# Fourteen of a block 1 layer's eighteen modulation units moved from the head slots to the norm and convolution mean slots, two a slot

## The chip, the cores and the metric

One Trainium2 (trn2) chip, of which the kernel uses 1 core. The metric is the device time of one execution in microseconds (us), lower is better. It is given as the median of several executions of one built kernel.

## What is computed

Two transformer-like blocks run one after the other on a sequence of 256 tokens of width 1024, in float32, each with two layers (`DEPTH = 2`). Cut to what matters here:

```python
def first_block(x, ...):
    for l in range(DEPTH):
        h = _rmsnorm(x, g_mix[l])
        proj = h @ w_in[l]                       # gates 4096, conv 512, three attentions 2560 columns
        y_a = _conformer_conv(a_in, ...)         # depthwise conv of 31 taps, layernorm, silu
        y_b = _neighbourhood_attn(norm(bq), norm(bk), bv, na_rpb[l])
        y_c = _dilated_attn(rope(norm(cq)), rope(norm(ck)), cv)
        y_d = _window_gqa_sink(rope(norm(dq)), rope(norm(dk)), dv, swa_sink[l])
        branch = einsum('bsnc,ncd->bsnd', stack(y_a, y_b, y_c, y_d), w_branch[l])
        gates = sigmoid(gate_pre + gate_b[l])
        x = x + sum(gates * branch, axis=2) @ w_out[l]
        x = x + _conv_ffn(_rmsnorm(x, g_ffn[l]), ...)
    return x

def second_block(x, c, ctx, c_ctx, w_mod, b_mod, ...):
    for l in range(DEPTH):
        m_x = silu(c) @ w_mod[l] + b_mod[l]      # modulation: 1024 x 9216, needs c alone
        m_c = silu(c_ctx) @ w_mod[l] + b_mod[l]
        ...                                      # FFN, MLA attention, FFN, all scaled by m_x, m_c
```

The modulation of block 2 depends on none of block 1's results, so it can be computed anywhere before block 2 needs it.

## The kernel before, in words

**Products.** A float32 weight tile of 1 MB (`raw`, a ring of `RAW = 4` slots) is loaded by SyncE's queue (L713), rounded by ScalarE into `whi` (helper `copy`, L1193, in `round_next`), and what the rounding left is taken by VectorE into `wlo` (L1542, in `rest_next`). TensorE then makes three products for every pair of 128-row tiles (L859 to L861 in `unit`). A *unit* of the phase `gates` is 48 such products of 256 columns into two PSUM banks `acc`. ScalarE takes the two results out with a tanh (L1374).

**Modulation.** `w_mod` is cut into 36 *modulation units* a layer, each 1 MB. A modulation unit skips the rounding: `mod_unit` (L946) multiplies `cond` by the raw tile, 8 small products into a bank; `mod_rows` (ScalarE, `copy`) copies the row to `mod_row`; `mod_turn` (TensorE, L955) turns it into columns in the same bank; `mod_out` (VectorE, L1661) adds the bias. A bank and a half of `mod_row` are used again two units later, so `mod_unit` waits for the `mod_out` of two units before. Half of layer 0's 36 units (of block 2's layer 0) are computed in block 1's layer 0, half in its layer 1; the other 36 lie in block 2's attention and are not touched.

**The slots.** Block 1's attention part is written out by hand as a list of slots (`slots_block1`), and every engine walks the same list. They are: six `prep` slots (prep 0 to prep 5), each the norm of two tiles of q or k, with rope from prep 2 on; a `mean` slot and a `var` slot for the layernorm behind the convolution; and fourteen `head` slots (head 0 to head 13), each with the scores of one head, the softmax of the one before and the value product of the one before that. Sixteen `gates` units are spread over them: prep 0, 2, 4 and mean have gates 0 to 3, heads 0 to 11 have gates 4 to 15. Within a slot each engine keeps its own written order:

- TensorE: in `prep` the sum of squares (L830), the gates unit, the rope product (L1042). In `head` the scores (L906), the turn (L955) and product (L946) of a modulation unit, the gates unit, in every second slot a further turn and product, then `weigh` (`op`, L926) and `turn_probs` (`ptp`, L915).
- ScalarE: in `prep` the squares (L1233), the root (`take_root`, L1245), the rounding of the next weights, the two tanh. In `head` the rounding, `exps` (L1286), `mod_rows`, the two tanh, the copies of `ptp` and `op`. Sqrt, tanh and exp need table loads (ACT_TABLE_LOAD) between them, exp and tanh together none.
- VectorE: in `prep` the reciprocal of the root (L1570), the scaling (L1587), `wlo`, the rope (L1771 to L1774). In `head` `peaks` (L1607 to L1618), `normalise` (L1636, L1640), `wlo`, `mod_out`, `br_lo` (L1653).

**Order of the loads.** `mod_order` puts each modulation tile into the stream of loads behind a gates tile; the ring of four slots is filled strictly in that order, and a slot is free when the tile four places before has been used.

**Eighteen units over the heads.** `mods_block1(l, k)` gives head k one unit, and heads 2, 4, 6 and 8 (`MOD_TWICE`) two. Their banks are `stat` and `rotp`, which no norm or rope needs during the heads.

```python
MOD_TWICE = (2, 4, 6, 8)
def mod_bank(u):
    return (stat, rotp)[u % 2]
```

## Time and profile before

| | |
|---|---|
| Median of 3 runs | 3140.37 us (3120.49 to 3142.45) |
| The profiled execution's own time | 3125.25 us |
| Its span, first to last instruction | 3123.5 us |
| TensorE busy | 2860.1 us (92%) |
| VectorE, ScalarE, GpSimdE busy | 1546.2, 1102.8, 70.6 us |
| Mean granted TensorE clock | 0.936 of full speed |

The profile is of one execution. The span leaves 1.75 us of the execution's time outside it. Times in rows of the trace count from the span's start. Block 1's layer 0 has its slots from about 99 to 287 us, layer 1 from about 641 to 828 us. A matmul's busy time is modelled and overlaps that of the next, so the distance between the starts of two rows is what a step costs.

### The profile page before, as it was taken

To read this page: it belongs to the slowest core of one execution; us is meant where nothing else is said; L and a number is where in the kernel's file an instruction comes from. 1 tells how busy PE (TensorE), PEld (TensorE's weight loads), DVE (VectorE), ACT (ScalarE), POOL (GpSimd) and SP (SyncE) were. 2 spreads that over 40 slices of the span, in tenths; PEclk is the share of its full clock that TensorE was granted. 3 is DMA by queue.
4 is the path that set the end of the run, shared out by engine and by line. 5 is a ranking of instruction groups with operands and counts; after the bars stand their busy time and mean duration, and the time that the engine had idled before them with its cause. 6 is when DMAs were issued, how large, how long until landed. Compare 5 with 4: busy or idle time off the path is not lost.

```text
span 3123.5 us, 41599 instructions
## 1 busy us (share of the span) xinstructions
PE 2860.1 (92%) x16697; PEld 2360.6 (76%) x16697; DVE 1546.2 (50%) x2230; ACT 1102.8 (35%) x1527; POOL 70.6 (2%) x97
## 2 busy tenths in 40 slices
PE   6899799889889989999799998999979999799897
PEld 6677799867779968888574565888858888656897
DVE  5755676775568553333433235333353333543655
ACT  4543464455346442121333223222132121433433
POOL 3000100100100000000000000000000000000000
PEclk9899899999989989999898698999989999789999
DMA  7376365627546532433234432242322423334563
GB/s 199 108 227 219 108 182 153 193 95 249 197 136 183 153 97 80 114 86 94 69 80 138 137 119 67 70 113 82 101 68 74 122 82 100 92 112 132 139 191 92
DMA packets 613569, 394.44 MB, mean 126 GB/s; under 512 B 47691, under 2 KB 609543, under 8 KB 613157
## 3 DMA queue, kind: packets, MB, share of 16 engines
q1 hardware_dynamic: 609424, 383.03, 41.6%
q0 software_dynamic: 2960, 7.75, 1.0%
q8 instruction: 112, 1.84, 0.3%
q10 hardware_dynamic: 1029, 1.47, 0.1%
q14 instruction: 44, 0.36, 0.0%
HBM read 391.16 MB, written 1.05 MB: 126 GB/s over the span
## 4 chain that ended last, share of the span: by engine, by line
PE 84%; DVE 10%; ACT 3%; issue 1%; DVEq 1%; DMA 0%; ACTq 0%; POOL 0%
PE acc L859 12%; PE acc L860 11%; PE acc L861 11%; PE scores L859 6%; PE scores L860 6%; PE scores L861 6%; PE scores L906 3%; PE acc L877 3%; PE acc L878 3%; PE acc L879 3%; PE scores L877 3%; PE scores L878 3%; PE scores L879 3%; PE op L926 2%; DVE rstd L1570 2%; DVE wlo L1542 2%
## 5 line engine op out<-in xcount | busy, mean ns | idle before, releaser
L1193 ACT ACTIVATE whi<-raw 128x2048 fp32r<-128x2048 f32 (+2 forms) x326 | 565.8, 1736 | 895.2 <-PE acc L861 287.3
L859 PE MATMUL acc<-h_hi,whi 128*128 128x256 f32 (+1 forms) x2372 | 801.5, 338 | 84.8 <-DVE h_lo L1581 48.3
L1542 DVE TENSOR_TENSOR wlo<-raw,whi 128x2048 fp32r<-128x2048 f32 (+2 forms) x325 | 674.6, 2076 | 214.5 <-ACT whi L1193 213.9
L860 PE MATMUL acc<-h_lo,whi 128*128 128x256 f32 (+1 forms) x2372 | 778.6, 328 | 0.0
L861 PE MATMUL acc<-h_hi,wlo 128*128 128x256 f32 (+1 forms) x2372 | 777.6, 328 | 0.0
L859 PEld LDWEIGHTS acc<-h_hi,whi 128*128 128x128 f32 x2372 | 462.9, 195 | 173.4 <-issue 78.4
L860 PEld LDWEIGHTS acc<-h_lo,whi 128*128 128x128 f32 x2372 | 465.9, 196 | 37.1 <-issue 2.5
L861 PEld LDWEIGHTS acc<-h_hi,wlo 128*128 128x128 f32 x2372 | 464.8, 196 | 37.4
L859 PE MATMUL scores<-h_hi,whi 128*128 128x256 f32 (+1 forms) x992 | 334.7, 337 | 0.0
L860 PE MATMUL scores<-h_lo,whi 128*128 128x256 f32 (+1 forms) x992 | 334.0, 337 | 0.0
L861 PE MATMUL scores<-h_hi,wlo 128*128 128x256 f32 (+1 forms) x992 | 333.7, 336 | 0.0
L859 PEld LDWEIGHTS scores<-h_hi,whi 128*128 128x128 f32 x992 | 186.6, 188 | 22.3 <-issue 0.2
L861 PEld LDWEIGHTS scores<-h_hi,wlo 128*128 128x128 f32 x992 | 186.8, 188 | 21.6
L860 PEld LDWEIGHTS scores<-h_lo,whi 128*128 128x128 f32 x992 | 186.7, 188 | 21.6
L877 PE MATMUL acc<-a_hi,whi 128*128 128x256 f32 (+1 forms) x528 | 181.2, 343 | 8.1 <-DVE wlo L1542 8.1
L878 PE MATMUL acc<-a_lo,whi 128*128 128x256 f32 (+1 forms) x528 | 180.4, 342 | 0.0
L879 PE MATMUL acc<-a_hi,wlo 128*128 128x256 f32 (+1 forms) x528 | 180.3, 341 | 0.0
L877 PE MATMUL scores<-a_hi,whi 128*128 128x256 f32 (+1 forms) x528 | 179.2, 339 | 0.0
L879 PE MATMUL scores<-a_hi,wlo 128*128 128x256 f32 (+1 forms) x528 | 178.8, 339 | 0.0
L878 PE MATMUL scores<-a_lo,whi 128*128 128x256 f32 (+1 forms) x528 | 178.8, 339 | 0.0
L1871 DVE TENSOR_TENSOR a_hi<-sg,acc 128x512 f32 (+3 forms) x48 | 29.9, 622 | 262.4 <-PE acc L861 262.4
L1871 DVE TENSOR_TENSOR a_hi<-sg,scores 128x512 f32 (+3 forms) x40 | 24.9, 622 | 221.8 <-PE scores L861 221.8
(274 smaller groups left out, 3305.3 us busy)
## 6 DMA issues: line engine op xcount, KB each, us to landing
raw<-in_ffn_w_in_dram SPq DMA_DIRECT2D x176, 512.0 KB, 5.0
raw<-in_w_mod_dram SPq DMA_DIRECT2D x72, 1024.0 KB, 5.1
raw<-in_w_in_dram SPq DMA_DIRECT2D x62, 1024.0 KB, 5.3
raw<-in_w_up_dram SPq DMA_DIRECT2D x88, 512.0 KB, 4.9
raw<-in_ffn_w_out_dram SPq DMA_DIRECT2D x64, 704.0 KB, 4.6
raw<-in_w_down_dram SPq DMA_DIRECT2D x32, 704.0 KB, 4.7
raw<-in_w_out_dram SPq DMA_DIRECT2D x16, 1024.0 KB, 5.3
raw<-in_w_branch_dram SPq DMA_DIRECT2D x8, 1024.0 KB, 6.4
```

Of the source, the lines that this page charges most:

```text
L859: pe.matmul(bank, wh, hi[:, c0 + k, 0:width], start=(k == 0), stop=False)
L860: pe.matmul(bank, wh, lo[:, c0 + k, 0:width], start=False, stop=False)
L861: ins = pe.matmul(bank, wl, hi[:, c0 + k, 0:width], start=False, stop=(k == ph.shape[0] - 1))
L877: pe.matmul(bank, wh, hi[:, c0 + k, 0:width], start=(k == 0), stop=False)
L878: pe.matmul(bank, wh, lo[:, c0 + k, 0:width], start=False, stop=False)
L879: ins = pe.matmul(bank, wl, hi[:, c0 + k, 0:width], start=False, stop=(k == FH - 1))
L906: ins = pe.matmul(bank[:, t * w:(t + 1) * w], q_, k_, start=(e == 0), stop=(e == len(terms) - 1))
L926: ins = pe.matmul(op_[job["rows"], 0:w], v, job["prt"][:, b % 2, kt * w:(kt + 1) * w], start=(kt == 0), stop=(kt == nk - 1))
L1193: return act.activation(out_, in_, ACT.Copy, **kw)
L1542: dve.tensor_tensor(wlo[:, s % 2, 0:el], raw[:, slot, 0:el], f32(whi[:, s % 2, 0:el]), ALU.subtract).then_inc(s_lo, 1)
L1570: dve.reciprocal(rstd[:, 0:w_], root[:, 0:w_]).then_inc(s_rstd, 1)
L1871: dve.tensor_tensor(hi, sg2[:, b, 0:T], bank_of(ph, j, 1, 4)[:, 0:T], ALU.mult).then_inc(s_accfree, 1)
```

## The change

Of a layer's eighteen modulation units, fourteen are now issued in the slots prep 0 to prep 5 and mean, two in each, and four in heads 1, 3, 5 and 7. In the prep and mean slots the units come at the end of the slot on TensorE; their copies, turns and outputs stand in the *next* slot (the list `late`). In the heads too, a unit is now issued at the end of its slot, and its copy, turn and output come in the next slot. Units in prep and mean slots use the banks `scores0` and `scores1`, which no attention uses there; the scores of head 0 now wait for their last output. The tiles stand earlier in the stream of loads.

Cut to its core (`...` marks what is left out):

```diff
-MOD_TWICE = (2, 4, 6, 8)
+MOD_HEADS = (1, 3, 5, 7)
...
+        rounded = 0
+        for (kind, k, gate), units in zip(slots_block1(), mods_block1(l)):
+            rounded = rounded if gate is None else gate + 1
+            behind = (f"1.{l}.gates", rounded) if rounded < 16 else (f"1.{l}.branch", 0)
+            given.setdefault(behind, []).extend((0, e) for e in units)
+            u += len(units)
...
+def mods_block1(l):
+    out_, u = [], l * MOD_HALF
+    for kind, k, gate in slots_block1():
+        units = 2 if kind in ("prep", "mean") else 1 if kind == "head" and k in MOD_HEADS else 0
+        out_.append(list(range(u, u + units)))
+        u += units
+    return out_
...
         def mod_bank(u):
+            if u < MOD_UNITS and u % MOD_HALF < MOD_HALF - len(MOD_HEADS):
+                return sp_[u % 2]
             return (stat, rotp)[u % 2]
...  TensorE
+                late = []
+                for (kind, k, gate), here in zip(slots1, mods_block1(l)):
...
-                            pe.wait_ge(s_rpbm, 4 * (l + 1))
+                            pe.wait_ge(s_modout, n("mod"))
                             scores(0, jobs[0])
...
-                    if kind == "head":
-                        mine = mods_block1(l, k)
-                        if k == 0:
-                            pe.wait_ge(s_cond, 2)
-                            pe.wait_ge(s_root, n("norm"))
-                        else:
-                            mod_turn()
-                        mod_unit(0, mine[0])
+                    for u in late:
+                        mod_turn()
                     if gate is not None:
                         unit(nm + "gates", gate, None, h1_hi, h1_lo, SEQ, plain(256))
-                    if kind == "head":
-                        for u in mine[1:]:
-                            mod_turn()
-                            mod_unit(0, u)
...
                     if kind == "head":
                         attend(jobs, k)
...
+                    for u in here:
+                        mod_unit(0, u)
+                    late = here
...  ScalarE
                         squares(norm_heads(l, k))
+                    if kind == "var":
+                        squares(norm_conv(l), [(s_conv, 2 * l + 2)])
+                    if kind != "head":
+                        for u in late:
+                            mod_rows()
+                    if kind == "prep":
                         take_root(norm_heads(l, k))
...
                     if kind == "head":
-                        mod_rows()
+                        for u in late:
+                            mod_rows()
+                    late = here
...  VectorE
                     if gate is not None:
                         rest_next(nm + "gates", gate, None)
-                    if kind == "head" and k >= 1:
+                    for u in late:
                         mod_out()
+                    late = here
```

TensorE, block 1's layer 0, from the sum of squares of prep 1 on. Before, where only the gates unit of prep 2 (its 48 products on `acc1` and `acc0` are left out here) stands between the sums of squares and the rope product:

```order
L830 MATMUL stat<-sq,shared 128x512 [waits s_root,s_sq] x2
...
L1042 MATMUL rotp<-qk,t1 128x512 [waits s_plain]
L830 MATMUL stat<-sq,shared 128x512 [waits s_root,s_sq]
L1042 MATMUL rotp<-qk,t1 128x512 [waits s_roped,s_plain]
L830 MATMUL stat<-sq,shared 128x512 [waits s_root,s_sq]
```

Now, the same place up to the sum of squares of prep 2 (its two turns and its gates unit follow):

```order
L836 MATMUL stat<-sq,shared 128x512 [waits s_root,s_sq]
L961 MATMUL scores0<-shared,mod_row 128x2 [waits s_modrow]
L961 MATMUL scores0<-shared,mod_row 128x2
L961 MATMUL scores1<-shared,mod_row 128x2 [waits s_modrow]
L961 MATMUL scores1<-shared,mod_row 128x2
L952 MATMUL scores0<-raw,cond 32x256 [waits s_modout,s_raw2]
L952 MATMUL scores0<-raw,cond 32x256 x7
L952 MATMUL scores1<-raw,cond 32x256 [waits s_modout,s_raw3]
L952 MATMUL scores1<-raw,cond 32x256 x7
L836 MATMUL stat<-sq,shared 128x512 [waits s_root,s_sq]
```

The sum of squares of prep 2 stood right behind that of prep 1; now it stands behind two modulation products that wait for VectorE (`s_modout`).

ScalarE, the same layer, from the squares of prep 1 to the root of prep 2. Before:

```order
L1233 ACTIVATE sq<-qk 128x512 [waits s_sum]
L1245 ACT_TABLE_LOAD [waits s_rstd]
L1245 ACTIVATE root<-stat,eps 128x512 [waits s_sum]
L1233 ACTIVATE sq<-qk 128x512 [waits s_sum]
L1245 ACTIVATE root<-stat,eps 128x512 [waits s_rstd,s_sum]
```

Now:

```order
L1237 ACTIVATE sq<-qk 128x512 [waits s_sum]
L1197 ACTIVATE mod_row<-scores0 128x256 [waits s_modmm]
L1197 ACTIVATE mod_row<-scores1 128x256 [waits s_modmm]
L1249 ACT_TABLE_LOAD [waits s_rstd]
L1249 ACTIVATE root<-stat,eps 128x512 [waits s_sum]
L1237 ACTIVATE sq<-qk 128x512 [waits s_sum]
L1197 ACTIVATE mod_row<-scores0 128x256 [waits s_modt,s_modmm]
L1197 ACTIVATE mod_row<-scores1 128x256 [waits s_modt,s_modmm]
L1249 ACTIVATE root<-stat,eps 128x512 [waits s_rstd,s_sum]
```

Each root now stands behind two copies that wait for the modulation products (`s_modmm`), and in prep 1 the table load stands behind them too.

TensorE in the heads, from the end of head 1 to the first product of the gates unit of head 2 (`ptp` of head 0, then the scores of head 3). Before:

```order
L915 MATMUL ptp<-shared,pr1 128x128 [waits s_turned,s_prob]
L915 MATMUL ptp<-shared,pr1 128x128 x3
L906 MATMUL scores1<-qk 128x256 [waits s_exp]
L906 MATMUL scores1<-qk 128x256
L955 MATMUL rotp<-shared,mod_row 128x2 [waits s_modrow]
L955 MATMUL rotp<-shared,mod_row 128x2
L946 MATMUL stat<-raw,cond 32x256 [waits s_modout,s_raw0]
L946 MATMUL stat<-raw,cond 32x256 x7
```

Now:

```order
L921 MATMUL ptp<-shared,pr1 128x128 [waits s_turned,s_prob]
L921 MATMUL ptp<-shared,pr1 128x128 x3
L952 MATMUL stat<-raw,cond 32x256 [waits s_modout,s_raw3]
L952 MATMUL stat<-raw,cond 32x256 x7
L912 MATMUL scores1<-qk 128x256 [waits s_exp]
L912 MATMUL scores1<-qk 128x256
L961 MATMUL stat<-shared,mod_row 128x2 [waits s_modrow]
L961 MATMUL stat<-shared,mod_row 128x2
```

Before, the turn belonged to the unit multiplied ahead of head 1's gates unit; now it belongs to the one multiplied just ahead of the scores, with only the scores between product and turn.

## Rows read from the trace of the kernel before

**Rows 1.** The page: the span, and the chain that ended last by engine.

```profile
span 3123.5 us, 41599 instructions
...
PE 84%; DVE 10%; ACT 3%; issue 1%; DVEq 1%; DMA 0%; ACTq 0%; POOL 0%
```

**Rows 2.** Windows: layer 0's preps, heads; layer 1's; 11 us of loads. The first line names the columns.

```profile
core 0: us, PE busy (x) PEld busy (x) DVE busy (x) ACT busy (x) POOL busy (x), PEclk, DMA share, GB/s
98.80:156.60 57.80, 44.27 (x249) 33.94 (x247) 42.39 (x35) 31.62 (x38) 0.00 (x0) 0.85 0.22 74
156.60:287.30 130.70, 127.71 (x1060) 103.72 (x1057) 67.33 (x141) 64.52 (x126) 0.00 (x0) 0.99 0.72 234
641.00:697.20 56.20, 41.25 (x247) 31.96 (x245) 41.73 (x33) 29.63 (x35) 0.00 (x0) 0.91 0.23 75
697.20:828.30 131.10, 127.67 (x1061) 104.02 (x1057) 67.37 (x141) 64.52 (x126) 0.00 (x0) 0.99 0.72 231
...
711.00:722.00 11.00, 11.00 (x101) 9.74 (x102) 5.20 (x9) 5.59 (x11) 0.00 (x0) 1.00 0.89 282
```

**Rows 3.** ScalarE's timeline, preps 0 and 1: start us, us, what, [idle before, releaser].

```profile
107.03 0.47 ACT L1374 ACTIVATE gates<-acc,par 128x256 f32<-128x256 f32 x1 [1.41 <-PE acc L861]
107.40 0.62 ACT L1233 ACTIVATE sq<-qk 128x512 f32<-128x512 f32 x1
108.03 1.28 ACT L1245 ACT_TABLE_LOAD   x1
109.33 0.69 ACT L1245 ACTIVATE root<-stat,eps 128x512 f32<-128x512 f32 x1
```

**Rows 4.** Timeline of VectorE: reciprocal and scaling of prep 1, `wlo`; then prep 5.

```profile
110.11 3.35 DVE L1570 RECIPROCAL rstd<-root 128x512 f32<-128x512 f32 x1 [1.59 <-ACT root L1245]
113.56 0.75 DVE L1587 SCALAR_TENSOR_TENSOR qk<-qk,par,rstd 128x512 f32<-128x512 f32 x1
...
118.52 2.29 DVE L1542 TENSOR_TENSOR wlo<-raw,whi 128x2048 fp32r<-128x2048 f32 x1
...
140.17 1.75 DVE L1570 RECIPROCAL rstd<-root 128x256 f32<-128x256 f32 x1
```

**Rows 5.** Timeline of TensorE in preps 2 to 4: rope product and sum of squares.

```profile
118.83 1.02 PE L1042 MATMUL rotp<-qk,t 128*128 128x512 f32 x2
...
127.11 2.08 PE L1042 MATMUL rotp<-qk,t 128*128 128x512 f32 x2 [5.92 <-DVE qk L1587]
128.98 1.92 PE L830 MATMUL stat<-sq,shared 128*128 128x512 f32 x2
```

**Rows 6.** Timeline of TensorE from head 4's end into head 5, and that unit's end.

```profile
205.45 1.08 PE L926 MATMUL op<-prt,v 128*64 128x256 f32 x4
206.46 0.66 PE L915 MATMUL ptp<-shared,pr 128*128 128x128 f32 x4
207.05 1.13 PE L906 MATMUL scores<-qk 64*128 64x256 f32 x4
208.34 0.61 PE L955 MATMUL stat<-shared,mod_row 128*128 128x2 f32 x4 [0.16 <-ACT mod_row L1193]
208.87 1.07 PE L946 MATMUL rotp<-raw,cond 128*32 128x256 f32 x16
209.87 0.39 PE L859 MATMUL acc<-h_hi,whi 128*128 128x256 f32 x1
...
215.76 1.08 PE L926 MATMUL op<-prt,v 128*64 128x256 f32 x4
```

**Rows 7.** Timeline of ScalarE in head 5.

```profile
210.35 0.91 ACT L1286 ACTIVATE pr<-sm,npeak 128x256 f32<-128x256 f32 x2 [0.27 <-DVE npeak L1618]
211.17 0.36 ACT L1193 ACTIVATE mod_row<-rotp 128x256 f32<-128x256 f32 x1
```

**Rows 8.** The page's DMA issues: the modulation tiles, us from issue to landing.

```profile
raw<-in_w_mod_dram SPq DMA_DIRECT2D x72, 1024.0 KB, 5.1
```

**Rows 9.** Timeline of TensorE in layer 1's head 9: product, gates unit, `op`.

```profile
792.44 1.07 PE L946 MATMUL rotp<-raw,cond 128*32 128x256 f32 x16 [1.03 <-DMA raw<-in_w_mod_dram]
...
800.84 1.08 PE L926 MATMUL op<-prt,v 128*64 128x256 f32 x4
```

More of the change, by code:

```diff
@@ L237, in mod_order @@
     for l in range(DEPTH):
-        for kind, k, gate in slots_block1():
-            if kind == "head":
-                behind = (f"1.{l}.gates", gate + 1) if gate is not None and gate < 15 else (f"1.{l}.branch", 0)
-                units = mods_block1(l, k)
-                given.setdefault(behind, []).extend((0, e) for e in units)
-                u += len(units)
+        rounded = 0
[4 more added lines that the diff above has]
+            u += len(units)
     assert u == MOD_UNITS
@@ L252, in mods_block2 @@
     return range(MOD_AHEAD) if l == 0 else range(MOD_AHEAD, MOD_UNITS)
-def mods_block1(l, k):
-    first = l * MOD_HALF + k + sum(1 for e in MOD_TWICE if e < k)
-    return list(range(first, first + (2 if k in MOD_TWICE else 1)))
+def mods_block1(l):
[5 more added lines that the diff above has]
+    return out_
 def slots_block1():
@@ L1045, in _ @@
                         attend(jobs, k)
-                mod_turn()
+                    if kind == "prep" and k == 0:
+                        pe.wait_ge(s_cond, 2)
+                        pe.wait_ge(s_rpbm, 4 * (l + 1))
+                    if kind == "head" and k == 0:
+                        pe.wait_ge(s_root, n("norm"))
+                    for u in here:
+                        mod_unit(0, u)
+                    late = here
                 n("job", 12)
@@ L1349, in _ @@
                 jobs = jobs_block1(l)
-                for kind, k, gate in slots1:
+                late = []
+                for (kind, k, gate), here in zip(slots1, mods_block1(l)):
                     if kind == "prep":
@@ L1727, in _ @@
                 jobs = jobs_block1(l)
-                for kind, k, gate in slots1:
+                late = []
+                for (kind, k, gate), here in zip(slots1, mods_block1(l)):
                     if kind == "prep":
@@ L1760, in _ @@
                         attend_rest(jobs, k)
-                        for u in mods_block1(l, k)[1:]:
-                            mod_out()
                     if kind == "prep":
@@ L1774, in _ @@
                             dve.tensor_tensor(pair, pair, rt, ALU.add).then_inc(s_roped, 1)
-                mod_out()
                 if l == DEPTH - 1:
```

5 lines of the change are left out of this document (removed).

## The prediction, written before the changed kernel had run

> **What bounds the kernel now.** I read the page first: 84% of the chain that ended last is TensorE, 10% VectorE, DMA nothing [rows 1]. So moving TensorE's work pays only where it moves into idle time of TensorE that nothing else needs. The windows by stage come next [rows 2]. They split each of block 1's layers in two. In the heads (130.70 us in layer 0, 131.10 in layer 1, from the first gates unit of head 0 to the first branch unit) TensorE is busy 127.7 us: the heads are bound by TensorE, and work taken out of them shortens them. In the prep, mean and var slots (57.80 and 56.20 us) TensorE is busy 44.27 and 41.25 us, VectorE 42.39 and 41.73: nobody is full, and the trace shows why. It is a ping-pong. ScalarE takes a root [rows 3], VectorE a reciprocal of 3.35 us and a scaling [rows 4], and TensorE sits idle for 5.92 us in front of a rope product that waits for the scaling [rows 5]. Before, this ping-pong ran partly ahead: as the order shows, a prep without a gates unit puts nothing between its own sum of squares and root and those of the next.
>
> **What the change takes out of the heads.** The number of modulation units is the same. One costs 1.00 us for the product (208.87 to 209.87) and 0.53 for the turn (208.34 to 208.87) [rows 6]. Fourteen leave: 14 x 1.53 = 21.4 us, of which about 0.4 was hidden in overlaps, so 21.0. The idle 0.9 us behind head 0's gates unit is covered (that unit starts later against the softmax than before), and a gates unit that ran at the half clock in the heads of each layer cost 1.5 us more; I count 1.3 of it as gone. Against that, in heads 12 and 13 the short chain of `op`, `ptp` and copies was partly filled by two units, and what they leave is idle, 1.1 us. Together -21.0 - 0.9 - 1.3 + 1.1 = -22.1 us a layer. At the most it is -23.6 (nothing hidden, 21.4 + 2.2); at the least, if the tail keeps all of its last two units' time (3.1 us), -20.
>
> **What it puts back into the heads.** In heads 2, 4, 6 and 8 a turn now stands right behind the scores, and its product only one place ahead of them. The turn needs the copy `mod_row`, and ScalarE makes that copy only after `exps` of this head. In head 5 of before the chain is: `op` ends about 0.07 us after `ptp` starts, so it ended at 206.53 [rows 6]; `exps` runs at 210.35, `mod_row` at 211.17 to 211.53 [rows 7]. The copy is there 5.0 to 5.2 us behind `op`. TensorE arrives at the turn after `ptp` 0.59, the product 1.00 and the scores 1.06 [rows 6], 2.6 us behind `op`. So it waits 2.6 us, four times: +10.4 us a layer. Behind the waiting turn stand the gates unit, `op` and `ptp`; their inputs are ready, so the wait is a plain loss. Before, the product lay a whole gates unit ahead of its turn, and the wait was 0.16 us [rows 6]. Bounds: 0 (if ScalarE's chain moves forward by as much) and 3.5 a time. The heads net: -22.1 + 10.4 = -11.7 us a layer.
>
> **What it does to the preps.** Each slot now closes a ring: the root stands behind the copies of the pair, these behind the pair's products, these behind the rope product and the `mod_out` of VectorE, these behind the scaling, and that behind the root. I add up from one pair's end to the next. The links, from rows:
> - Last product to next root: 1.72 us where ScalarE loads a table (copy 0.4, load 1.29, rest latency) [rows 3]; 1.1 where it does not, since TensorE's sum of squares (1.02 [rows 5]) now stands behind the pair.
> - Root to the end of scaling: 0.78 (109.33 to 110.11), 3.45 (to 113.56), 0.75: 4.98, and what follows on VectorE starts 0.08 sooner, 4.90 behind the root [rows 3, 4]. `wlo` 2.2 (2.29, less the overlap with the next) [rows 4]; a `mod_out` is some 0.15, which is small either way.
> - A pair of products 2.07, a turn 0.55, a gates unit 5.85 (209.87 to 215.76) [rows 6], a rope product 1.0 [rows 5].
>
> Layer 0, starting from the end of gates unit 0 at 106.99 (its tanh starts at 107.03 [rows 3]):
> - prep 0: two products, to 109.0.
> - prep 1: 1.72 + 4.90 + 0.2 + 2.07 = 8.9, to 117.9.
> - prep 2: here TensorE itself is the longest: sum of squares 1.05, two turns 1.1, unit 5.85, rope 0.9, pair 2.0 = 10.9, to 128.8. (VectorE needs 1.1 + 4.90 + 2.2 + 0.15 = 8.4 and is ready before the rope product ends.)
> - prep 3: 1.72 + 4.98 + 1.0 + 2.07 = 9.8, to 138.6.
> - prep 4, like prep 2: 10.9, to 149.5.
> - prep 5, 256 wide (reciprocal 1.75 [rows 4]): 1.72 + 2.9 + 0.7 + 2.07 = 7.4, to 156.9.
> - mean: mean product 1.0, turns 1.1, unit 5.85, pair 2.0 = 9.95, to 166.8.
> - var: 1.72 to the root, 4.35 through reciprocal, scaling, bias and the last `mod_out`, for which head 0's scores now wait, 1.05 for them: to 173.9.
>
> Before, head 0's gates unit began at 156.6 [rows 2]. So the preps grow by 17.3 us in layer 0. Layer 1 took some 0.8 us less than layer 0 for the same stretch and gets the same links, so +18.1: mean +17.7. Bounds: nothing of the ring lies on the path, then only the `mod_out` and copies, about +2; or each step is serial, every slot with its unit, rope, reciprocal and pair one behind the other, +30.
>
> One rule of the Trainium skill speaks on a link of this ring. The trace shows the table load at 108.03 with 1.28 us and the root at 109.33, 0.02 us behind it [rows 3], so a link costs 1.30. ScalarE: Activation LUTs, section What ACT_TABLE_LOAD costs, says that each switch also costs a drain of about 1380 ns, 2.66 us in all. By that, four links a layer (prep 1, 3, 5, var) would be 1.38 longer and the kernel 11 us slower than my sum; by the row they are not. I go by the row.
>
> **The clock.** The granted clock is 0.85 in layer 0's preps against 0.99 in the heads [rows 2], and the rows say what comes before it falls: behind 5.92 us of idle the rope product takes 2.08 instead of 1.02 and the sum of squares 1.92 instead of 1.02 [rows 5], the level of 1.2 instead of 2.4 GHz. That is 2.0 us. In my schedule TensorE has idle stretches of 4.8 us (prep 1), 4.6 (prep 3), 2.9 (prep 5) and 3.9 (var). I charge three of them with 2.0 us each, since what follows (pair, sum of squares, turns, unit) is now on the path: +6.0 a layer, bounds 0 and 11. In the heads a gates unit behind a wait of 1.03 us and a product took some 7.4 us (the product starts at 792.44, so the unit at 793.44, `op` at 800.84) [rows 9] instead of 5.89: 1.5. The four new waits of 2.6 us stand in a stretch of light work (`op`, `ptp`, product, scores, turn); I charge half of them: +3.0, bounds 0 and 6.
>
> **Loads.** The preps now take 14 modulation tiles beside their gates tiles. Walking the ring of four slots with 5.1 us from issue to landing [rows 8], each tile is there 3 us or more before its product: the closest is the second tile of prep 1, whose slot comes free with the `wlo` of gates 1 at about 108.5, so landed at 113.6, and used at 117. The heads have held 234 GB/s over 130 us and 282 over 11 us [rows 2]; 14 + 4 MB in some 75 us is 250. I charge nothing. What it costs without that cover: see the rivals.
>
> **The sum.** A layer: +17.7 (preps) - 11.7 (heads) + 6.0 + 3.0 (clock) = +15.0 us; two layers +30.0. On the profiled execution's 3125.25 that is 3155.3. This execution is 15 us below the median of 3140.37 in a spread of 22 us; I put the change on the median: 3170.4 us, +0.96%. Block 2's modulation is untouched, and the branch stage starts with the same waits.
>
> **The rivals.** A measurement of this kernel can tell about 1%, 31 us, from no change.
> - *The preps hide the pairs* (the other side). If the ring is not closed in practice because ScalarE's root of the next slot mostly waited for VectorE anyway, the preps grow by 2 us and the heads still give 11.7 less 3.0: -6.7 a layer, 3127 us. For it: 13 to 15 us of TensorE idle in each layer's preps [rows 2]. Against: they lie in front of products that wait for the scaling, and the order puts each root behind the pair of the slot before. It decides once the root of prep 2 comes within 2 us of prep 1's scaling. With the waits in the heads also missing it is -1.0% and more.
> - *The clock does not fall more often than before*: only 6.0 a layer, +12: 3152 us. For it: the pairs also fill idle time.
> - *The turns in the heads do not wait*: 10.4 + 3.0 less a layer, +3: 3144 us. Against: rows 7.
> - *The loads bound the preps*: 18 tiles one behind the other at 5.1 [rows 8] are 92 us against the 75 of my schedule, +17 a layer: 3204 us. Against: 282 GB/s with several in flight [rows 2].
> - *Every light stretch ends at the half clock*, the upper bounds of both clock terms, +8 a layer: 3186 us.
>
> Of the clock, TensorE: Matmul & The Clock Gate, section HAM oscillation, warns that idle gaps before bursts of products keep bringing back the half clock; that is this last rival's mechanism, and the trace agrees for the gap of 5.92 us.
>
> **How the numbers follow.** Chances: forecast 0.56, preps hide 0.12, clock stays 0.13, turns do not wait 0.06, loads 0.06, full clock cost 0.07. The forecast's own range is +18 to +42 us, and half of it lies above +31. Slower by over 1%: 0.29 of the forecast + 0.06 + 0.07 = 0.42. Faster by over 1%: 0.05, the far part of the first rival. The rest, 0.53, is within 1%. The range leaves out most of the first rival and the loads: 3143 to 3195.
>
> **What would show each step.** In the changed profile: the time from gates unit 0's end to head 0's gates unit (49.6 before, 67 to 73 if right); the heads from there to the first branch unit (130.7 before, 119 to 122); turns waiting for ScalarE's `mod_row` about 2.6 us, four times a layer; the root of prep 2 waiting for TensorE's sum of squares, some 8 us behind the root of prep 1; the granted clock in the preps near 0.85 still; TensorE waiting for no modulation tile. The prediction is wrong if the preps grow by less than 10 us a layer, or if the turns find their row ready.

## The result, and the profile after

The changed kernel takes 3165.21 us (median of 4 runs, 3163.92 to 3177.59); the kernel before, run beside it, 3130.43 (4 runs, 3117.01 to 3142.45). The ratio is 1.0121, with a 95% interval of 1.0063 to 1.0179: slower by about 1.2%. The forecast was 3170.4, with 3143 to 3195 as its range. A total can land in a range that wide by luck, so the terms matter more than the total, and two of them were not right. Of all executions reported here two ran in a slower state, at a mean granted clock of 0.81 (3300.64 us, one of the kernel before, and 3333.87 us, one of e8_fill_preps), and no median or ratio counts them.

The profiled execution of the changed kernel took 3165.55 us. Its page, beside [rows 1]:

```profile
span 3163.8 us, 41601 instructions
...
PE 85%; DVE 9%; ACT 3%; issue 1%; DVEq 1%; ACTq 0%; POOL 0%
```

The span is 40.3 us longer for two more instructions, and the shares of the chain have hardly moved. The page alone can't say where the time went. The windows can. I divided each layer of block 1 at the same three instructions in every trace: the end of gates unit 0, the first product of head 0's gates unit, the first product of the branch stage. Windows of the kernel before with these bounds, preps of layer 0, preps of layer 1, then everything behind layer 1's heads (the columns are those of [rows 2]; its heads are in [rows 2], as 130.70 and 131.10 us):

```profile
106.99:156.59 49.60, 36.07 (x195) 27.34 (x195) 35.50 (x29) 25.47 (x31) 0.00 (x0) 0.83 0.25 85
648.33:697.17 48.84, 33.89 (x195) 25.71 (x194) 35.59 (x29) 25.35 (x31) 0.00 (x0) 0.90 0.27 87
828.27:3123.45 2295.18, 2130.52 (x11076) 1709.34 (x11076) 1015.49 (x1419) 705.67 (x939) 16.73 (x13) 0.93 0.38 108
```

The same windows of the changed kernel: preps and heads of layer 0, preps and heads of layer 1, the rest.

```profile
106.72:180.07 73.35, 55.75 (x458) 38.71 (x458) 39.69 (x48) 33.27 (x47) 0.00 (x0) 0.83 0.81 258
180.07:311.02 130.95, 116.03 (x794) 99.49 (x793) 63.38 (x121) 57.76 (x110) 0.00 (x0) 0.91 0.39 129
669.34:743.01 73.67, 55.62 (x458) 38.82 (x458) 39.67 (x48) 33.37 (x47) 0.00 (x0) 0.84 0.80 257
743.01:874.19 131.18, 116.25 (x795) 99.72 (x793) 63.39 (x122) 57.68 (x110) 0.00 (x0) 0.91 0.39 129
874.19:3163.75 2289.56, 2117.36 (x11076) 1703.92 (x11076) 1015.12 (x1418) 705.79 (x939) 16.75 (x13) 0.93 0.38 108
```

Three things are to be read here. The preps grew by 23.8 and 24.8 us a layer. The heads, in whose windows the trace has 266 products fewer, did not shrink at all: 130.95 and 131.18 us. Their TensorE is busy 11.7 us less than before and idle for the rest, and the granted clock in them fell from 0.99 to 0.91. And the rest of the kernel, which the change doesn't touch, is 8.6 us shorter (5.6 behind layer 1's heads, 2.7 between the two layers, 0.3 before), so 48.9 us of loss in the two layers show as 40.3.

**The ring in the preps.** TensorE's waits in layer 0's preps; the fence shows every stretch of TensorE there with an idle time in front of it, and the three rows around the first:

```profile
108.51 1.13 PE L836 MATMUL stat<-sq,shared 128*128 128x512 f32 x2
109.47 0.95 PE L961 MATMUL scores<-shared,mod_row 128*128 128x2 f32 x8
115.55 3.64 PE L952 MATMUL scores<-raw,cond 128*32 128x256 f32 x32 [5.12 <-DVE mods L1671]
119.12 2.08 PE L836 MATMUL stat<-sq,shared 128*128 128x512 f32 x2
...
137.46 2.07 PE L1039 MATMUL rotp<-qk,t 128*128 128x512 f32 x2 [4.96 <-DVE qk L1597]
...
157.70 1.22 PE L1039 MATMUL rotp<-qk,t 128*128 128x256 f32 x2 [3.30 <-DVE qk L1597]
...
178.06 2.09 PE L912 MATMUL scores<-qk 64*128 64x256 f32 x8 [4.22 <-DVE mods L1671]
```

Four waits, 5.12, 4.96, 3.30 and 4.22 us: the four of the forecast's walk (4.8, 4.6, 2.9, 3.9). None waits for a tile from DMA. Behind each, the next products run at the half clock in this profile: a pair of modulation products takes 3.64 us instead of 1.93, and the sum of squares 2.08 instead of 1.13. ScalarE, beside [rows 3], shows the same ring from its side:

```profile
108.65 0.38 ACT L1197 ACTIVATE mod_row<-scores 128x256 f32<-128x256 f32 x1 [0.48 <-PE scores L952]
109.05 1.28 ACT L1249 ACT_TABLE_LOAD   x1
110.35 0.69 ACT L1249 ACTIVATE root<-stat,eps 128x512 f32<-128x512 f32 x1
...
117.54 0.38 ACT L1197 ACTIVATE mod_row<-scores 128x256 f32<-128x256 f32 x1 [5.99 <-PE scores L952]
119.25 0.38 ACT L1197 ACTIVATE mod_row<-scores 128x256 f32<-128x256 f32 x1 [1.32 <-PE scores L952]
121.23 0.69 ACT L1249 ACTIVATE root<-stat,eps 128x512 f32<-128x512 f32 x1 [1.60 <-PE stat L836]
```

ScalarE is idle for 5.99 us until the pair's first product arrives, and the next root follows the last one by 10.9 us (110.35 to 121.23). Between them VectorE's reciprocal and scaling take the same times as in [rows 4], and then come the two small outputs that free the banks:

```profile
111.13 3.35 DVE L1580 RECIPROCAL rstd<-root 128x512 f32<-128x512 f32 x1 [2.88 <-ACT root L1249]
114.58 0.75 DVE L1597 SCALAR_TENSOR_TENSOR qk<-qk,par,rstd 128x512 f32<-128x512 f32 x1
115.25 0.22 DVE L1671 TENSOR_TENSOR mods<-scores,par 128x4 f32<-128x4 f32 x2
```

So the pair starts only once these outputs are written (115.25 to 115.47), behind a reciprocal of 3.35 us that has nothing to do with them.

**The heads.** TensorE at the turn of head 2, beside [rows 6]:

```profile
195.57 1.13 PE L912 MATMUL scores<-qk 64*128 64x256 f32 x4
199.19 0.61 PE L961 MATMUL stat<-shared,mod_row 128*128 128x2 f32 x4 [2.49 <-ACT mod_row L1197]
...
200.25 0.41 PE L865 MATMUL acc<-h_hi,whi 128*128 128x256 f32 x1
...
204.81 0.28 PE L865 MATMUL acc<-h_hi,whi 128*128 128x256 f32 x1
```

TensorE waits 2.49 us for `mod_row`, whose copy stands behind `exps` on ScalarE, as in [rows 7] (the first line is one of the two exponentials of `exps`):

```profile
197.78 0.51 ACT L1290 ACTIVATE pr<-sm,npeak 128x256 f32<-128x256 f32 x1 [0.26 <-DVE npeak L1628]
198.78 0.36 ACT L1197 ACTIVATE mod_row<-stat 128x256 f32<-128x256 f32 x1
```

The four waits of layer 0 are 2.49, 2.63, 2.63 and 3.06 us, together 10.8. And the gates unit behind each pays once more: its first products come every 0.21 us, later ones every 0.12 (0.41 and 0.28 us each, as they overlap). From first gates product to `op`, the units of heads 2, 4, 6 and 8 take 7.4, 7.4, 8.4 and 8.0 us; those of the other heads 5.8 to 5.9. Head 0's unit, behind the wait of 4.22 us, starts at the half clock too and takes 7.1 to the next scores.

### The profile page after: what moved, and what is told of

Same layout as the page of the kernel before. It is cut to its first block, busy times and chain, and to the rows that moved or that the text cites. A ratio compares the mean times of both kernels' runs of the same rounds, so it can differ in the third digit from the quotient of the medians.

```text
span 3163.8 us, 41601 instructions
## 1 busy us (share of the span) xinstructions
PE 2864.0 (91%) x16697; PEld 2370.7 (75%) x16697; DVE 1547.5 (49%) x2230; ACT 1105.2 (35%) x1527; POOL 69.7 (2%) x97
## 4 chain that ended last, share of the span: by engine, by line
PE 85%; DVE 9%; ACT 3%; issue 1%; DVEq 1%; ACTq 0%; POOL 0%
PE acc L865 12%; PE acc L867 12%; PE acc L866 12%; PE scores L865 6%; PE scores L867 6%; PE scores L866 6%; PE scores L912 4%; PE acc L883 3%; PE acc L885 3%; PE acc L884 3%; PE scores L885 3%; PE scores L883 3%; PE scores L884 3%; PE op L932 3%; DVE rstd L1580 2%
## 5 line engine op out<-in xcount | busy, mean ns | idle before, releaser
L883 PE MATMUL acc<-a_hi,whi 128*128 128x256 f32 (+1 forms) x528 | 180.3, 341 | 8.0 <-DVE wlo L1552 8.0
L1880 DVE TENSOR_TENSOR a_hi<-sg,scores 128x512 f32 (+3 forms) x40 | 24.8, 621 | 220.7 <-PE scores L867 220.7
```

The costliest lines, as they stand in the source:

```text
L883: pe.matmul(bank, wh, hi[:, c0 + k, 0:width], start=(k == 0), stop=False)
L1880: dve.tensor_tensor(hi, sg2[:, b, 0:T], bank_of(ph, j, 1, 4)[:, 0:T], ALU.mult).then_inc(s_accfree, 1)
```

## The experiments

All times are medians; ratios are against the kernel before on the same chip, with 95% intervals. Kernels e1 to e4 share 32 runs of it (3125.23 us); e6, e7, e8 and the changed kernel again share 16 (3121.19); e5 stands against 7 (3115.28). Stages come from the one profiled execution of each, and without another word "the changed kernel" means its first profile.

### The heads: product and copy put back ahead of the gates unit

e1_heads_old moves the four head units back to the place they had before, within the same slots; the preps stay as changed.

```diff
  TensorE
                     for u in late:
                         mod_turn()
+                    if kind == "head":
+                        if k == 0:
+                            pe.wait_ge(s_root, n("norm"))
+                        for u in here:
+                            mod_unit(0, u)
                     if gate is not None:
                         unit(nm + "gates", ...)
...
-                    for u in here:
-                        mod_unit(0, u)
+                    if kind != "head":
+                        for u in here:
+                            mod_unit(0, u)
  ScalarE
                     if kind == "head":
-                        for u in late:
+                        for u in here:
                             mod_rows()
```

> Undoes the order in the heads alone: the four units of heads 1, 3, 5, 7 are multiplied ahead of their own slot's gates unit and copied in that slot, so that their turn comes a whole gates unit later. The preps stay as changed. Theory (the turns' waits, and the half clock behind them, eat the heads' gain): no turn waits, the gates units of heads 2, 4, 6, 8 take 5.95 us instead of 7.45 to 8.4, the heads take 112 us a layer instead of 131, and the kernel 3165 - 38 = 3127 us. Rival (the clock falls in the heads because they hold less work in all, whatever the turns do): waits gone but the units stay at 7.5 to 8.4, heads 121, 3146 us.

Measured: 3132.52 us, ratio 1.0027 (1.0002 to 1.0052). Layer 0's heads (layer 1's take 111.19):

```profile
180.10:291.77 111.67, 107.56 (x794) 91.28 (x793) 63.43 (x121) 57.68 (x110) 0.00 (x0) 0.99 0.45 151
```

The same 794 products take 111.7 us instead of 131.0, at a clock of 0.99 instead of 0.91; the preps stay at 73.1 and 71.5. No turn waits, and the units of heads 2, 4, 6, 8 take 5.9 us. So the position of four units alone costs 19.3 and 20.0 us, and with it gone nearly all of the kernel's loss is gone: what is left of the move is a gain in the heads (19 to 20 us a layer) that the preps eat (22 to 24).

### Only the copy moved

e2_copy_first leaves every product where the change put it and moves ScalarE's copy, in the heads too, to the front of its slot, ahead of `exps`.

```diff
  ScalarE
-                    if kind != "head":
-                        for u in late:
-                            mod_rows()
+                    for u in late:
+                        mod_rows()
...
-                    if kind == "head":
-                        for u in late:
-                            mod_rows()
```

> Leaves TensorE's order as changed and moves only ScalarE's copy of the row in the heads: first in the slot, ahead of the rounding and exps. Theory (the turn waits for the copy because exps stand ahead of it): the copy is done 2.3 us behind op, before TensorE comes at 2.6, so no wait, heads 112 us a layer, 3127 us, like the run that undoes the heads' order. Rival (the product too near the turn is what costs, wherever the copy stands): a wait of 1 us or more stays, heads 120 or more, 3145 us.

Measured: 3137.53 us, 1.0044 (1.0024 to 1.0065). TensorE at the turn of head 2, and the window of layer 0's heads:

```profile
195.71 1.13 PE L912 MATMUL scores<-qk 64*128 64x256 f32 x4
196.76 0.61 PE L961 MATMUL stat<-shared,mod_row 128*128 128x2 f32 x4
```

```profile
179.98:291.74 111.76, 107.65 (x794) 91.38 (x793) 63.42 (x121) 57.40 (x110) 0.00 (x0) 0.99 0.45 151
```

The turn follows the scores at once, and the heads are as short as in e1. This is the cleanest run of the study: products, transfers and their order on TensorE are those of the changed kernel, and one instruction's place on ScalarE is worth 19.2 and 19.6 us a layer. It fells the rival by which less work in the heads itself brings the half clock: the units take 5.9 us with the same little work around them. I expected 3127 us for the kernel; all other stretches of this profile together are 8.6 us longer than in the changed kernel's, so of 38.8 us gained in the heads its span shows 30.2.

### The preps: the ring opened

e3_preps_open puts the pair of a prep slot ahead of the rope product on TensorE, and the outputs of the previous pair ahead of the reciprocal on VectorE. The heads stay as changed.

```diff
  TensorE
                         unit(nm + "gates", ...)
+                    if kind == "prep":
+                        for u in here:
+                            mod_unit(0, u)
                     if kind == "prep" and k >= 2:
                         pe.wait_ge(s_plain, ...)
...
-                    for u in here:
-                        mod_unit(0, u)
+                    if kind != "prep":
+                        for u in here:
+                            mod_unit(0, u)
  VectorE
                     if kind == "prep":
+                        for u in late:
+                            mod_out()
                         scale_norm(norm_heads(l, k))
...
-                    for u in late:
-                        mod_out()
+                    if kind != "prep":
+                        for u in late:
+                            mod_out()
```

> Opens the ring in the preps and leaves the heads as changed: TensorE multiplies a prep's pair before the rope product, VectorE makes the outputs of the pair before ahead of the reciprocal, so the pair no longer waits for the scaling. Theory (the ring root, scaling, output, pair, copies, root is what makes the preps 24 us longer): from gates unit 0's end to head 0's gates unit some 60 us instead of 73.5, of 49 before; kernel 3165 - 27 = 3138 us. Rival (work that TensorE, VectorE and ScalarE have more of in the preps is what costs, or the loads): still 70 us or more, 3158 us or more.

Measured: 3152.39 us, 1.0097 (1.0059 to 1.0135). Windows of layer 0's preps and heads and of layer 1's preps:

```profile
107.06:171.31 64.25, 53.32 (x459) 39.86 (x459) 40.12 (x48) 33.30 (x47) 0.00 (x0) 0.88 0.92 292
171.31:304.59 133.28, 118.35 (x794) 101.82 (x793) 63.43 (x121) 57.73 (x110) 0.00 (x0) 0.89 0.38 128
662.65:724.68 62.03, 50.55 (x458) 36.87 (x458) 40.14 (x48) 33.53 (x47) 0.00 (x0) 0.95 0.95 304
```

The preps fall by 9.1 and 11.6 us (7.1 and 9.3 against the changed kernel's second profile, below), where I expected some 13. That is the ring: the same instructions, in an order in which the pair no longer waits for the reciprocal. The fall holds some of the half clock too, since the granted clock rises from 0.83 to 0.88 in layer 0, and the two edits, on TensorE and on VectorE, were not tried one by one. Of the waits left in layer 0 before head 0's scores, the two longest are 2.33 us for a scaling, in front of a rope product, and this one for DMA, in front of the second unit of prep 1:

```profile
113.91 1.07 PE L952 MATMUL scores<-raw,cond 128*32 128x256 f32 x16 [2.14 <-DMA raw<-in_w_mod_dram]
```

DMA moves 292 and 304 GB/s there, so once the ring is open the loads are next in line. The heads came out 2 us longer than in the changed kernel (units of 8.6, 8.4, 8.3 and 8.0 us); of the 20.7 us that the two preps gave, the medians show 12 to 13.

### Both together

e4_both has the edits of e1 and e3 together, and no others.

> Both: the ring in the preps opened and the heads' old order. If the two costs add up: 3165 - 38 - 27 = 3100 us, 1% under the kernel before (preps 60 us, heads 112 us, against 49 and 131). If the loads bound the preps once the ring is open, or the heads then wait for loads, 3115 us or more.

Measured: 3117.03 us, 0.9989 (0.9966 to 1.0012): no difference from before that can be told. Layer 0's preps and heads:

```profile
107.02:167.12 60.10, 50.48 (x458) 36.80 (x458) 39.96 (x48) 33.45 (x47) 0.00 (x0) 0.94 0.98 310
167.12:278.97 111.85, 107.74 (x795) 91.47 (x793) 63.43 (x121) 57.70 (x110) 0.00 (x0) 0.98 0.46 154
```

In the stages the two parts add up: 172.0 us for layer 0's preps and heads, 180.3 before. The idea of the change is sound, then, in the two layers together by 14 us; more than a third of that is lost in the rest of this execution, where the stretch behind layer 1's heads took 2300.6 us, 5.4 more than before. I expected 3100 us, with 27 for the ring, and e3 had given 20.7. Even with the ring open the preps are 10.5 and 13.2 us longer than before. What makes up that rest was not separated; in layer 0 TensorE is busy 14.4 us more than before (50.48 against 36.07) and waits 2.00, 1.16 and 0.32 us for modulation tiles.

### A rival for the ring: the copies behind the root

If the roots are late because each stands behind two copies on ScalarE, it is enough to take the root first. e5_copies_after_root does that, the order on TensorE and VectorE stays as changed.

```diff
  ScalarE
-                    if kind != "head":
-                        for u in late:
-                            mod_rows()
                     if kind == "prep":
                         take_root(norm_heads(l, k))
                     if kind == "var":
                         take_root(norm_conv(l))
+                    if kind != "head":
+                        for u in late:
+                            mod_rows()
```

> The changed kernel with ScalarE's order in the preps and var turned round: the root first, the copies of the pair behind it. Theory (what closes the ring is that the pair waits for VectorE's output behind the scaling, and the sum of squares stands behind the pair; the copies ahead of the root are a small link): in prep 1, 3, 5 and var the root comes 0.6 us sooner, in prep 2 and 4 not at all, the turns come later by as much, preps 70 to 73 us a layer of 73.5, kernel within 5 us of the changed one (3164). Rival (the copies ahead of the root close the ring): preps 62 or less, 3140 us.

Measured: 3180.31 us, 1.0182 (1.0110 to 1.0254). ScalarE's roots of preps 1 and 2:

```profile
110.83 0.69 ACT L1249 ACTIVATE root<-stat,eps 128x512 f32<-128x512 f32 x1 [0.63 <-PE stat L836]
...
121.27 0.69 ACT L1249 ACTIVATE root<-stat,eps 128x512 f32<-128x512 f32 x1 [8.68 <-PE stat L836]
```

```profile
107.88:182.81 74.93, 59.39 (x459) 40.68 (x459) 39.69 (x48) 31.98 (x47) 0.00 (x0) 0.81 0.78 253
880.42:3193.85 2313.43, 2142.72 (x11076) 1713.44 (x11076) 1014.01 (x1418) 705.52 (x939) 17.61 (x13) 0.93 0.37 107
```

Prep 1's root is 0.7 us sooner behind gates unit 0 (2.95 us instead of 3.63), but the next is still 10.4 us behind it (10.9 in the changed kernel), because it waits 8.68 us for TensorE's sum of squares. The ring runs through TensorE and VectorE; the copies are not the link that closes it. The preps took 74.9 and 76.5 us, longer than I expected (70 to 73): the turns now wait about 1 us each for their copies, and the gates units of preps 2 and 4 took 7.2 to 7.4 us instead of 5.8. How much each of the two cost was not separated.

### The clock in the heads: the waits filled

The wait of a turn and the half clock behind it come together. To part them, e6_fill_heads issues 20 products of 256 columns just ahead of each of the four turns, into a bank that is free there. Nobody reads them; they only keep TensorE busy during the wait.

```diff
+FILL = 20
...
+                    if kind == "head" and late:
+                        pe.wait_ge(s_lo, by_name[nm + "gates"].s0 + gate + 1)
+                        pe.wait_ge(s_modout, n("mod") - 1)
+                        slot_ = (by_name[nm + "gates"].s0 + gate) % 2
+                        for e in range(FILL):
+                            pe.matmul((stat, rotp)[n("mod") % 2][:, 0:256], whi[:, slot_, (e % 8) * 256:(e % 8) * 256 + P],
+                                      h1_hi[:, e % 8, :], start=True, stop=True)
                     for u in late:
                         mod_turn()
```

> The changed kernel with 20 products of 256 columns, whose result nobody reads, put between the scores and the waiting turn in heads 2, 4, 6, 8 (2.4 us, as long as the wait). The computation is unchanged otherwise. Theory (the idle wait is what brings the half clock to the gates unit behind it): the turn comes no sooner, but those units take 5.95 us instead of 7.45 to 8.4, heads 131 - 8 = 123 us a layer, kernel 16 us below the changed one. Rival (the clock falls for another reason, so the fill changes nothing): heads 131, kernel as changed.

Measured: 3158.50 us, 1.0121 (1.0079 to 1.0163). TensorE at the turn of head 2 (the lines of this kernel are one further on), and layer 0's heads:

```profile
193.28 1.13 PE L913 MATMUL scores<-qk 64*128 64x256 f32 x4
194.34 2.63 PE L1036 MATMUL rotp<-h_hi,whi 128*128 128x256 f32 x20
196.91 0.61 PE L962 MATMUL stat<-shared,mod_row 128*128 128x2 f32 x4
```

```profile
177.84:300.30 122.46, 117.73 (x875) 100.74 (x873) 63.42 (x121) 57.79 (x110) 0.00 (x0) 0.99 0.42 138
```

The turn comes at the same distance from the scores as with the wait (3.63 us from the scores' start, 3.62 in the changed kernel). The units are back at 5.9 us, the clock at 0.99, and the heads 8.5 and 8.9 us shorter. That is the price of the half clock behind four waits, and the remaining 10.8 us (122.46 less e1's 111.67) are the waits themselves. As a time for the whole kernel most of this gain doesn't show: I expected 16 us, and the median is 5.4 below that of the changed kernel on the same chip (3163.92). In this profile the stretch behind layer 1's heads was 12.3 us longer than in the changed kernel's first profile and 9.0 longer than in its second; why is open.

### The clock in the preps: the waits filled

e8_fill_preps does the same in the slots prep 1, prep 3, prep 5 and var, where the four waits of the preps are: 36, 34, 22 and 30 such products behind the turns, into `rotp`, read by nobody.

```diff
                     for u in late:
                         mod_turn()
+                    fill, g_ = {("prep", 1): (36, 1), ("prep", 3): (34, 2), ("prep", 5): (22, 3),
+                                ("var", 0): (30, 4)}.get((kind, k), (0, 0))
+                    if fill:
...
+                        for e in range(fill):
+                            pe.matmul(rotp[:, 0:256], whi[:, s_ % 2, (e % 8) * 256:(e % 8) * 256 + P],
+                                      h1_hi[:, e % 8, :], start=True, stop=True)
```

> The same kind of fill in the preps alone: 36, 34, 22 and 30 such products behind the turns of prep 1, prep 3, prep 5 and var, where TensorE sits idle for 3.3 to 5.1 us in the changed kernel. Theory (the prediction's clock term): preps 73.5 - 6.5 = 67 us a layer, which is the prediction's count at full clock, kernel 13 us below the changed one. Rival (the ring's links are longer than counted and the clock costs nothing on the path): 73 us.

Measured: 3161.18 us, 1.0142 (1.0088 to 1.0196). Layer 0's preps:

```profile
106.79:172.13 65.34, 62.64 (x580) 50.58 (x580) 39.67 (x48) 32.32 (x47) 0.00 (x0) 1.00 0.90 290
```

With the clock at 1.00 throughout, the preps take 65.3 and 65.9 us. My walk of the ring, which is at the full clock, gave 49.6 + 17.3 = 66.9. The difference to the changed kernel is what the clock costs there: 8.0 and 7.8 us by its first profile, 6.0 and 5.5 by its second (below); I had charged 6.0. The heads, not filled here, took 132.3 and 132.6, some 1.4 more than in the changed kernel. I expected the kernel 13 us below the changed one. Its median is 2.7 below, and with ratios of 1.0142 and 1.0145 the two can't be told apart: what the clock costs in the preps is read from the stage alone.

### The changed kernel once more

> The changed kernel itself, on the chip of the runs beside it, so that they can be compared with it: 3165 us, preps 73.5 and heads 131 us a layer.

Measured: 3163.92 us, 1.0145 (1.0098 to 1.0191). Its preps took 71.37 and 71.33 us and its heads 130.93 and 130.49, against 73.4, 73.7, 131.0 and 131.2 in the first profile. So one profile fixes the preps to about 2 us and the heads to under 1. In layer 0 the waits are the same to 0.01 us, and the whole difference of 2 us lies in the time that the same 458 products are busy, 53.78 instead of 55.75: the stretch at the half clock has another length each time, and behind the wait of 3.30 us the rope product ran at full clock here (0.70 us instead of 1.22).

### The last outputs ahead of the reciprocal of `var`

In e4, head 0's scores wait 4.22 us for the last outputs of the last pair, which stand behind the reciprocal of `var`. e7_var_first is e4 with these outputs ahead of it.

```diff
  VectorE
                     if kind == "var":
+                        for u in late:
+                            mod_out()
                         scale_norm(norm_conv(l))
...
-                    if kind != "prep":
+                    if kind not in ("prep", "var"):
                         for u in late:
                             mod_out()
```

> The kernel with the open ring and the old heads, and in the var slot too VectorE makes the outputs ahead of the reciprocal, so that head 0's scores, which wait for the last output, can go 4 to 5 us sooner, while the layernorm still runs. Expected: TensorE's wait of 4.2 us ahead of the scores gone, the gates unit behind it at full clock, scores of head 2 bound by the softmax of head 0 instead: 3 to 5 us a layer, 3117 - 8 = 3109 us. If the softmax of head 0 bounds all of it: 3117.

Measured: 3106.58 us, 0.9943 (0.9921 to 0.9966). Head 0's scores, and the windows of layer 0's preps and heads and layer 1's preps:

```profile
166.27 1.14 PE L912 MATMUL scores<-qk 64*128 64x256 f32 x8 [0.35 <-DVE mods L1678]
```

```profile
106.89:167.34 60.45, 53.49 (x459) 39.86 (x459) 37.33 (x43) 30.79 (x45) 0.00 (x0) 0.89 0.89 282
167.34:278.52 111.18, 106.14 (x794) 89.81 (x793) 66.35 (x127) 60.10 (x112) 0.00 (x0) 1.00 0.52 169
636.55:693.92 57.37, 49.69 (x460) 36.38 (x459) 37.34 (x43) 31.01 (x45) 0.00 (x0) 0.97 0.94 300
```

The wait of 4.22 us is down to 0.35, head 0's gates products start at the full clock, and the kernel is 0.6% faster than before and 1.8% faster than the changed one, with the same fourteen units in the same slots. I expected 3 to 5 us a layer over e4. Layer 1 gained 5.7 and layer 0 only 0.3: there the gates unit of prep 2 took 7.7 us in this profile, against 5.9 in e4's, and a rope product waited 2.33 us that had not waited in e4.

## Why the prediction was right in its sign and wrong in two steps

- **The walk of the ring in the preps (+17.7 a layer, and +6.0 for the clock).** Right. Sum 23.7; measured 23.8 and 24.8 in the first profile, 21.8 and 22.5 in the second. Both terms are shown apart: e8 without the half clock gives 65.3 where the walk has 66.9, and the clock is worth 5.5 to 8.0 where I charged 6.0. That the ring is on the path is shown by e3 (opened: -9.1 and -11.6) and by e5 (its rival: root to root still 10.4). It is not all of the growth: e4, with the ring open, keeps 10.5 and 13.2 us of it. The root of prep 2 was to wait for TensorE's sum of squares, "some 8 us behind the root of prep 1". It did wait for it, 10.9 us behind; the 8 us were at the full clock, and the pair (3.64 instead of 2.07) and the sum of squares (2.08 instead of 1.13) at the half clock give 2.5 of the 2.9 that lack.
- **The waits of the turns (+10.4 a layer).** Right: 10.8, in four waits of 2.49 to 3.06. That the copy stands behind `exps` is the cause: e2 moves it alone, and the waits are gone.
- **What the change takes out of the heads (-22.1 a layer).** Mis-sized. e1 has the removal without the waits, and its heads are 19.0 us shorter than before in layer 0 (130.71 to 111.67) and 19.9 in layer 1. Two steps of this sum failed. I let heads 12 and 13 keep only 1.1 us of their two units' time. From the start of `op` in head 11 to the first branch product it was 278.78 to 287.30 = 8.5 us before and is 302.51 to 311.02 = 8.5 us now, so the tail kept all 3.1 us, 2.0 more than I counted.

```profile
302.51 1.08 PE L932 MATMUL op<-prt,v 128*64 128x256 f32 x4
305.82 1.05 PE L932 MATMUL op<-prt,v 128*64 128x256 f32 x4 [1.64 <-DVE br_lo L1663]
```

  And I counted one product twice. Head 0's product stood in front of that head's gates unit, outside the window of the heads; the walk of the preps, which ends at 173.9 against 156.6, has it already. That is 1.0 us, and -22.1 becomes -19.1. Trace of the kernel before:

```profile
155.59 1.07 PE L946 MATMUL stat<-raw,cond 128*32 128x256 f32 x16
...
166.35 0.58 PE L859 MATMUL acc<-h_hi,whi 128*128 128x256 f32 x1
```

  The 1.3 us for a gates unit at the half clock did go: it was head 1's in layer 0 (7.0 us from 166.35 on, 5.8 now) and head 9's in layer 1 (7.4, now 5.9). But head 0's unit, at the full clock before, starts at the half clock now, behind the wait of 4.22 us.
- **The clock in the heads (+3.0 a layer).** This is the step that failed most. I charged half of the four waits with 1.5 us each, the excess of one unit behind one wait of 1.03 us [rows 9]. In the trace every one of the four waits, in both layers, is followed by a unit at the half clock, with an excess over 5.9 of about 1.5, 1.5, 2.5 and 2.2 us. Two of the turns took 0.88 us instead of 0.47 up to the first gates product, which makes it 8.4, over my upper bound of 6.0. e6 measures the same by another way: 8.5 and 8.9. Two mistakes, then: "half of them" had no row behind it, and the price came from a wait shorter than those to be priced. The rival that had each light stretch end at the half clock was nearer here than my forecast.
- **Together.** Heads -8.7 forecast, +0.2 and +0.1 measured, so the sign "119 to 122" for the heads failed (131): 2 to 3 us too much taken out, 5 to 6 too little for the clock, 0.4 for the waits. All three errors point the same way, so the two layers lost 48.9 us where I had 30.0. The kernel's total hides that: the untouched rest gave 8.6 us back in this profile, and the forecast stood on a median of 3140.37 that further runs of the kernel before put at 3115 to 3130. That 3170.4 lies so near 3165.2 is luck, two errors of opposite sign: the change costs 34.8 us by the first runs and 42.7 by the later ones, not 30, and the base was 10 to 25 us too high.
- **The rivals.** *The preps hide the pairs*: wrong, the ring closed. *The clock does not fall more often*: wrong, by e6 and e8 it costs 14 to 17 us a layer. *The turns do not wait*: wrong. *The loads bound the preps*: wrong for this kernel, no product waits for a modulation tile in the preps at 258 GB/s; single products do once the ring is opened (2.1 us in e3, at 292 GB/s). *Every light stretch at the half clock*: right for the heads, where even its bound of 6 was too low; in the preps every wait ended there in the first profile, but at 5.5 to 8.0 us the cost stayed nearer my 6 than its 11.
- **The table load.** The root follows the load in 0.02 us again (109.05 + 1.28 to 110.35). The drain of about 1380 ns that the Trainium skill (ScalarE: Activation LUTs, section What ACT_TABLE_LOAD costs) adds to each switch shows in neither kernel, and the walk without it fits.

## What to carry to other kernels

Work that is moved into an engine's idle time costs nothing only if its hand-offs (product, copy, turn, output) do not run through the chain that made the idle time. Write down on each engine what stands in front of each step, and keep a long unit between a product and what reads it. Here the same fourteen units in the same slots make the kernel 1.2% slower or 0.6% faster, by where the copy stands and whether two tiny outputs come ahead of a reciprocal of 3.35 us. And price a new wait twice, once as idle time and once as the slow clock of what follows, from a row with a wait at least as long.

## What the runs showed of the hardware that I had not expected

- The half clock behind waits of 2.5 to 3.1 us was no matter of chance. Such waits between light products brought it 16 times out of 16 in the heads of the changed kernel's two profiles, and cost about 1.5 to 2.5 us each, beside the wait itself. Behind shorter ones it was: in the kernel before, a wait of 0.85 us behind head 0's unit was followed by a unit of 7.0 us in layer 0 and of 5.8 in layer 1. The Trainium skill (TensorE: Matmul & The Clock Gate, section HAM oscillation) describes idle waits for DMA in front of bursts of products that bring back the half clock each time. The trace agrees, for waits that no DMA caused, and shows that 20 products nobody reads (2.63 us, e6) remove it.
- Windows with the same instructions differ between profiles by as much as some of the stages that I was measuring. Behind layer 1's heads, all these kernels run the same 11,076 products; the stretch took 2289.6 us in the changed kernel, 2292.8 in the same kernel again, 2295.2 before, 2300.6 in e4, 2301.8 in e6 and 2313.4 in e5. In e5 the products there are busy for 2142.7 us, in the changed kernel for 2117.4: the products themselves took longer, and the mean granted clock of the whole execution was 0.923 against 0.931. That points to the clock, but why it falls more often in one kernel than in another, and whether it goes with the kernel or with the execution, stays open. For a change that sits in 10% of a kernel, the stage in the trace is the sharper measure, and the total the blunter.
- The loads nearly kept up: layer 0's preps drew 85 GB/s before, 258 with the fourteen units, without a wait of TensorE for them, and 310 in e4, which moves the same tiles in less time and where TensorE waited 3.5 us in all for them.
